# Slot weights earlier, and the next gate subtraction ahead of the gate row, in a fused MoE backbone step

## The reference, cut to what matters

```python
gate = jnp.einsum('btd,edf->btef', h, w_eg)
up = jnp.einsum('btd,edf->btef', h, w_eu)
a = jax.nn.silu(gate) * up * combine.astype(h.dtype)[..., None]
return jnp.einsum('btef,efd->btd', a, w_ed)
...
x = x + ga2 * moe(h, w_router, b_router, w_eg, w_eu, w_ed)
```

## Time and profile before

| quantity | value |
|---|---|
| median of 3 runs | 1050.28 us |
| profiled execution | 1045.33 us, span 1043.5 us |
| TensorE busy | 994.8 us, 95% of the span |
| VectorE busy | 690.9 us, 66% |
| ScalarE busy | 447.3 us, 43% |
| GpSimd busy | 214.2 us, 21% |
| chain that ended last, by engine | PE 82%, DVE 7%, ACT 4%, DMA 2% |
| mean granted TensorE clock | 0.988 |

### The profile page before, as it was taken

The page is one execution under the profiler, slowest core; times in us unless marked ns, Lnnn a source line. Parts: engine busy times, 40 slices in busy tenths (PEclk is TensorE's granted clock), DMA queues, the critical chain, the costliest instruction groups (busy, mean ns, idle before and its releaser), DMA issues.

```text
span 1043.5 us, 18887 instructions
## 1 busy us (share of the span) xinstructions
PE 994.8 (95%) x6283; PEld 803.5 (77%) x6284; DVE 690.9 (66%) x1130; ACT 447.3 (43%) x883; POOL 214.2 (21%) x240
## 2 busy tenths in 40 slices
PE   6899999989999999999989999988899999999997
PEld 3799999989999988789975677666566666666665
DVE  3544887156698852438986554668777777777778
ACT  3443223245322223868982222222454545454534
POOL 3030000000000000303491000001335352535414
PEclk9999999999999999999999999999999999999999
DMA  9953433222434212232246323256688899989666
GB/s 364 350 198 130 151 122 142 84 99 84 147 132 143 84 67 92 85 115 68 66 112 241 115 94 122 102 197 268 229 260 282 272 282 286 320 259 303 164 171 274
DMA packets 58301, 184.58 MB, mean 177 GB/s; under 512 B 7780, under 2 KB 20710, under 8 KB 52102
## 3 DMA queue, kind: packets, MB, share of 16 engines
q1 hardware_dynamic: 48920, 151.02, 40.2%
q0 software_dynamic: 7632, 27.79, 11.3%
q10 hardware_dynamic: 1696, 5.10, 1.2%
HBM read 149.73 MB, written 34.16 MB: 176 GB/s over the span
## 4 chain that ended last, share of the span: by engine, by line
PE 82%; DVE 7%; ACT 4%; DMA 2%; issue 2%; SPq 2%; POOL 0%; POOLq 0%; ACTq 0%; DVEq 0%
PE psum L1435 42%; PE psum L1377 31%; PE psum L1708 2%; DMA RC<-in_w_ada 2%; PE psum L1301 1%; SPq L534 1%; DMA RW<-h_scratch,idxc 1%; PE psum L1392 1%; PE psum L1600 1%; ACT RE L1170 1%; PE psum L1730 1%; PE psum L1550 1%; ACT RA L1180 1%; DVE RE L2243 1%; ACT RW L1143 1%
## 5 line engine op out<-in xcount | busy, mean ns | idle before, releaser
L1377 PE MATMUL psum<-input_parts,weight_parts 128*128 128x320 f32 x2208 | 340.3, 313 | 2.9 <-DVE input_parts L1849 2.9
L1377 PEld LDWEIGHTS psum<-input_parts,weight_parts 128*128 128x128 f32 x2208 | 326.4, 189 | 11.8 <-issue 6.9
L972 ACT ACTIVATE weight_parts<-RW 128x1024 fp32r<-128x1024 f32 x46 | 48.7, 1058 | 226.0 <-PE psum L1377 215.0
L1856 DVE TENSOR_TENSOR weight_parts<-RW,weight_parts 128x1024 fp32r<-128x1024 f32 x46 | 56.3, 1225 | 115.1 <-ACT weight_parts L972 114.9
L1435 PE MATMUL psum<-expert_parts,row_of_slot 128*128 128x512 f32 x377 | 123.6, 395 | 2.2 <-DVE slot_parts L2394 1.1
L1435 PE MATMUL psum<-RB,RW 128*128 x270 | 121.9, 598 | 2.4 <-ACT heads_weight L1228 1.4
L1435 PEld LDWEIGHTS psum<-RB,RW 128*128 128x128 f32 x270 | 49.5, 191 | 56.2 <-issue 56.2
L1435 PEld LDWEIGHTS psum<-expert_parts,row_of_slot 128*128 128x128 f32 x377 | 70.7, 188 | 25.0 <-issue 10.6
L780 POOL TENSOR_TENSOR RE<-RE,RA 2x2304 f32<-2x2304 f32 (+1 forms) x2 | 9.0, 4512 | 349.6 <-DMA RA<-in_b_ada 349.5
L1435 PE MATMUL psum<-expert_parts,heads_weight 128*128 128x512 f32 x162 | 65.8, 460 | 0.0
L2413 DVE TENSOR_TENSOR expert_parts<-RB,expert_parts 128x1024 fp32r<-128x1024 f32 x54 | 63.5, 1218 | 2.0 <-ACT expert_parts L1249 1.2
(11 more groups left out here) (398 smaller groups left out, 1684.3 us busy)
## 6 DMA issues: line engine op xcount, KB each, us to landing
RB<-in_w_exp SPq DMA_DIRECT2D x48, 1024.0 KB
RW<-in_w_in SPq DMA_DIRECT2D x46, 512.0 KB, 4.2
RW<-in_w_ada SPq DMA_DIRECT2D x34, 512.0 KB, 3.4
RA<-in_w_ada SPq DMA_DIRECT2D x10, 512.0 KB, 14.2
RW<-gm_scratch SPq DMA_DIRECT2D x20, 256.0 KB, 3.4
h_scratch<-RE SPq DMA_DIRECT2D x10, 512.0 KB, 2.6
acc_scratch<-RA SPq DMA_DIRECT2D x10, 512.0 KB, 3.6
RB<-acc_scratch SPq DMA_DIRECT2D x10, 512.0 KB, 7.6
```

The lines of the kernel that those rows point to most:

```text
L972: nc.scalar.activation(spl[:, r, 0], raw[:, r], ACT.Copy).then_inc(whi_ok, 1)
L1377: last = nc.tensor.matmul(psum[:, 2 * r + g, 0:GW], spl[:, r, wv, k], hT[:, xv, k, g * GW:(g + 1) * GW], start=(k == 0 and wv == 0 and xv ...
L1856: nc.vector.tensor_tensor(spl[:, r, 1], raw[:, r], spl[:, r, 0].bitcast(F32), ALU.subtract).then_inc(wlo_ok, 1)
```

## The change

Nothing is computed otherwise; VectorE's instructions come in another order. Three things move:

1. Before the loop, the helper `slot_weights` is cut in three. The first part (the weights' split and `blkw`) comes ahead of the first `gate_low`. The second (`slot_rows`, with `idxS`) stays after the first `x_low`. The third (`gate_difference`) moves behind `gate_low` of block 1.
2. The first `product` comes ahead of `slot_weights_in`.
3. In the block loop `gate_low` of the next block comes ahead of `gate_rows` and `scaled_rows` of this one. The two blocks written out ahead of the loop and those behind it keep their order.

```diff
             last.then_inc(onehot, 1)
 
+        def slot_rows():
             then(nc.vector.tensor_scalar(wsum[:, 0:1], tokid[:, 0:1], float(T), None, ALU.add))
...
             nc.vector.tensor_tensor(idxS[:, :], eidf, padrow, ALU.add).then_inc(route_ok, 1)
 
+        def gate_difference():
             dve.wait_ge(rows_b, 16 * 10)
             then(nc.vector.tensor_tensor(ga2[:, 0], ga2[:, 0], ga2[:, 1], ALU.subtract))
...
         for b in range(2):
             dve.wait_ge(h2_out[b], STORED)
+        slot_weights()
         gate_low(0, slice(0, 1), SPLIT0 + 1)
         x_low(0, 1)
-        slot_weights()
+        slot_rows()
         down_low(0, slice(0, 1), SPLIT0 + 2)
+        product(0, 1)
         slot_weights_in()
-        product(0, 1)
         x_low(1, 2)
         gate_low(1, slice(1, 2), SPLIT0 + 4)
+        gate_difference()
...
                 product(1 - j, i * 2 + (4 + j))
+                gate_low(j, bass.ds(i * 2 + (4 + j), 1), i * 6 + (SPLIT0 + 13 + 3 * j))
                 out_rows(j, i * 2 + (2 + j), bass.ds(i * 2 + (2 + j), 1))
-                gate_low(j, bass.ds(i * 2 + (4 + j), 1), i * 6 + (SPLIT0 + 13 + 3 * j))
```

## The result

The changed kernel takes 1052.59 us (median of 20 runs, 1047.49 to 1059.04) against 1049.62 us for the kernel before (20 runs, 1044.01 to 1052.19). The ratio is 1.0037, with a 95% interval of 1.0022 to 1.0053: some 3.9 us slower, with an interval of 2.3 to 5.6. The forecast had the sign, and the time lies in its range, but it said +9.9 us.

The account below looks back on a forecast made before the run. The prediction took TensorE alone to bound the loop, at 10.23 us per block. The start's -0.8 us and the loop's +10.7 us gave +9.9 us, on 1050.28 us a forecast of 1060.2 us, range 1051.5 to 1065.

Parts of the forecast that it names:

- What bounds the kernel: Block loop: TensorE alone, 10.23 us per block; VectorE's order can win nothing there, only deliver in time or late.
- S+g+1.53: Loop: forecast start of gate_low; S is the product's start, g the delay from it to gate_high's start.
- The rule that the prediction weighed: A semaphore after each VectorE instruction costs nothing extra; by it the loop would lose some 8.5 us, not 10.7.
- the cover to watch: Loop: x_low ends 0.71 us before TensorE's split weight load of gate_up, taken as its slack.
- g - 0.54 us per plain block: Loss per block without a TensorE stall, from late x_low; g is product start to gate_high start: 0.43 at 0.97.
- +10.7 us: Loop's total loss: 10.1 us in 17 plain blocks, 0.6 us in the five where TensorE already stalls.
- the loop is covered: Rival: x_low arrives in time, so the loop costs nothing; 1049.5 us, no change; chance 0.10.
- the rows' scatter starts some 2.9 us later per block: Loop: the scaling ends at 6.8 instead of 3.9 us after the product's start; no cost in the forecast's sum.
- own stall: Loop: about one block in four has an extra stall of TensorE's, 0.33 to 0.55 us, swallowing most of the loss.
- The start, -0.8 us: Before the loop: idxS comes one register load earlier, so block 2's gather does too; bounds -3.6 to 0.
- what the prediction took for the clock: Start: a shorter gather wait might keep TensorE at 2.4 GHz, up to 1.7 us more; nothing counted.
- The rival of late gathers: Loop: gathers move by up to 2.9 us; five missing by 1 us and more add 5 us, 1065; chance 0.12.

Follow-up runs that it names:

- before_oneload: Kernel before, TensorE dropping the `need` register load and waiting for gate_low ahead of the plain matmuls instead: 1131.44 us, ratio 1.0782 to the kernel before.
- loop_oneload: Kernel before with the new loop order, TensorE dropping the `need` load and waiting for gate_low ahead of the plain matmuls: 1118.58 us, ratio 1.0661 to before.
- loop_only: Kernel before with only the block loop's new order, gate_low ahead of gate row and scaling: 1054.09 against 1048.55 us, ratio 1.0031.
- scatter_late: Kernel before with one more GpSimd wait, for the next block's x_low, ahead of add_rows in the loop: 1052.70 against 1048.96 us, ratio 1.0043.
- start_only: Changed start with the block loop in its old order, against the kernel before: 1047.51 against 1048.55 us, ratio 0.9997.
- after_hoist: Changed kernel with TensorE's two gate_up register loads read ahead of a_trans, against the kernel before: 1050.15 against 1049.61 us, ratio 1.0007.
- start_warm: Changed start, old loop, 26 filler matmuls on TensorE ahead of the loop, against the kernel before: 1050.36 against 1049.61 us, ratio 1.0005.

## Why the prediction was right or wrong

**What bounds the kernel.** Right: TensorE alone, and VectorE's order can win nothing in the loop. The rows show why the earlier gate_low is worthless, it already had 1.5 us of slack, and `before_oneload` against `loop_oneload` shows that it is worth 12.9 us where it has none.

**VectorE's times.** Right within 0.3 us in the block shown: gate_low at S+2.67 (forecast S+g+1.53 = 2.57), x_low's end at S+7.92 (7.65). The pair of gate row and scaling takes 1.50 us from start to start (774.28 to 775.78), where the prediction had 1.32; without a wait the same kind of instruction takes 1.20 (775.78 to 776.98). The rule that the prediction weighed, that a semaphore after each instruction costs nothing extra (the Trainium skill, VectorE: DVE Perf Modes, The DRAIN you can't avoid), does not agree with this trace for this pair.

**The step that failed.** "TensorE begins its split matmuls of gate_up with the weight load at 775.27, and for it the program waits for x_low and gate_low. x_low is there 0.71 us earlier (774.56). That is the cover to watch." The x_low that ends there is not the one that this gate_up waits for. Count it out in the program: behind product p, VectorE makes x_low p+2, while TensorE's gate_up of that stretch waits for `xl_ok` p+1, made a block earlier. The first step of TensorE that waits for x_low p+2 is `x_trans` of the next block, ahead of that block's gate_up. In the changed kernel these transposes are loaded at 782.42, 4.56 us behind the end of x_low at 777.86; that is its real cover, and not 0.71 us. So the g - 0.54 us per plain block, and with it the whole +10.7 us, has no place in the kernel. The seven blocks of the loop without a gap took 10.13 to 10.24 us; a period of 10.2 us in plain blocks is what the prediction had named as what would refute it. The rival "the loop is covered" was right on this point.

**What took its place.** A term that the sum put at nothing. That "the rows' scatter starts some 2.9 us later per block" was seen (it is 2.2 us in most blocks, S+5.8 to S+8.0), and it was weighed only by who waits for its results. It does its harm without being waited for: TensorE's two register loads, between the row transposes and the plain matmuls, are slow in many blocks when a scatter started 2 to 5 us ahead of them. In the trace this is the 5.3 us over the loop, in the times 3.3 us by the ratio (`loop_only`). `scatter_late` brings slow loads and loss back without the change. Hoisting the loads takes the stalls away, but not the whole distance between the orders: some 3 us stay, beside late gathers. The prediction also took the "own stall" of 0.41 us at 781.97 as TensorE's own and constant; it was the same effect, and the best hint at it.

**The start, -0.8 us.** idxS came earlier as forecast, 14.34 us behind L2320 (715.95 to 730.29) in place of 15.09 (716.60 to 731.69). In the times it does not show: 0.9997 for `start_only`. In the traces the granted clock was 0.5 for 6.83 us from 738.6 in the changed kernel, for 3.41 us in that of before, and the ten plain matmuls behind block 2's transposes took 7.47 us against 5.39, which is more than 0.8 us; but `loop_only` with the old start also had 6.83 us, and `after_hoist` with the new start 3.41. So the length is not the change's doing, and nothing in the times speaks against what the prediction took for the clock, nothing.

**The rival of late gathers.** Half right. The changed kernel's trace has none that TensorE waits for. With the loads hoisted they occur and cost 0.4 to 2.8 us each, with the order of before too; single ones of 5.3 to 7.2 us, with the clock at 0.5 for 3.41 or 6.83 us behind them, stand in the traces of `loop_only`, `start_only` and `start_warm`.

**The size.** The sign and the range came out right for another reason than the one given, which is luck. A sum of exact rows is no better than the pairing of who waits for whom.

What stays open: by what path the scatter slows a register load. The loads read their value from a tile in the cores' memory (`eidI`, `offI`). The Trainium skill (DMA: Bandwidth & Descriptors, Latency and other measured facts) offers as its best guess for another slow spot that the descriptor rings of GpSimd's DMAs lie in that memory, and that all 16 engines' fetches from them make its ports busier. No run here shows that path. Nor is every case explained: in the changed kernel two blocks (S at 929.46 and 970.96) behind a scatter as late as the others had loads of 0.30 to 0.33 us. Two more (939.59 and 981.20), with the scatter only 1.1 us ahead of S, had fast loads at 1.9 and 2.6 us behind it, so later is not always worse. And by what path the new order costs some 3 us with the loads hoisted is not settled.

## What to carry to other kernels

When a wait is given a price, count semaphore values by hand to find which iteration's result is waited for; a result that lies just ahead of its seeming reader in the timeline may be the one for the next block. A gap marked "issue" on the bounding engine can be work of its sequencer: look at its register loads, and read them ahead of the last wait, where other work covers them (0.3% here, for two lines moved). A transfer that nobody waits for can still have a cost by where it starts. And when a fix removes the stalls that a change made, compare the changed and the unchanged kernel with the fix in both: here the stalls went, and most of the distance stayed.

## What the runs showed of the hardware

- A register load by TensorE's sequencer takes 0.30 us undisturbed. It took up to 1.56 us in the changed kernel (1.59 in `start_only`), and over 0.6 us only where it began 2.1 to 4.9 us behind the start of a GpSimd scatter (125 of 624 loads in fourteen traces). Of the changed kernel's 46 loads in 23 blocks 25 took over 0.6 us.
- Other engines have slow loads too: in the changed kernel, from 765 to 1003 us, 7 of ScalarE's 90, 2 of VectorE's 44 and 5 of SyncE's 21 took over 0.6 us.
- The scatter's issue on GpSimd takes 1.61 us at S+5.8 and 2.40 us at S+8.0; the mean over the kernel went from 1.79 to 2.30 us.
- The granted clock behind TensorE's idle time at the start stood at 0.5 (1.2 GHz) for 3.41 us in some executions and for 6.83 us in others, with either start.
